# A hybrid encoder trunk on one core: the prologue in another order

## The reference

```python
c_act = jax.nn.silu(c)
for l in range(DEPTH):
    mod = c_act @ ada_w[l] + ada_b[l]
    sh1, sc1, gt1, sh2, sc2, gt2 = [m[:, None, :] for m in jnp.split(mod, 6, axis=-1)]
    h = rms_norm(x) * (1 + sc1) + sh1
    z = h @ w_in[l]
    ...  # z feeds latent attention with a rotary key, and a bidirectional RWKV-7 mixer
    x = x + gt1 * (jnp.concatenate([y_mla, y_rwkv], axis=-1) @ w_out[l])
    h = rms_norm(x) * (1 + sc2) + sh2
    x = x + gt2 * conv_ffn(h, ffn_w_up[l], ffn_conv_w[l], ffn_conv_b[l], ffn_w_down[l])
return rms_norm(x, final_norm)
```

## Time and profile before

| | us |
|---|---|
| median of 3 runs (lowest, highest) | 2013.53 (2013.17, 2016.87) |
| the profiled execution | 2015.64 |
| its span, first instruction to last | 2013.7 |
| TensorE's matmuls busy | 1702.9 (85%) |
| VectorE busy | 1066.8 (53%) |
| ScalarE busy | 726.9 (36%) |
| GpSimd busy | 293.2 (15%) |

### The profile page before, as it was taken

The page is one execution under the profiler, slowest core; times in us unless marked ns, Lnnn a source line. Parts: engine busy times, 40 slices in busy tenths (PEclk is TensorE's granted clock), DMA queues, the critical chain, the costliest instruction groups (busy, mean ns, idle before and its releaser), DMA issues.

```text
span 2013.7 us, 27787 instructions
## 1 busy us (share of the span) xinstructions
PE 1702.9 (85%) x11192; PEld 1259.4 (63%) x11192; DVE 1066.8 (53%) x1533; ACT 726.9 (36%) x1159; POOL 293.2 (15%) x124
## 2 busy tenths in 40 slices
PE   0897874888888899999989978568877989999997
PEld 0584432666655688887857834256655768888785
DVE  7254458777533776763333244677772254544333
ACT  1434233455442323232233343445545143232322
POOL 1242000000002122121223400000000222121120
PEclk9999895787788999999999989677788989999999
DMA  6254020000023345452213310000000312222222
GB/s 272 85 177 158 14 84 15 2 2 2 2 105 125 125 173 202 177 198 84 86 62 103 95 64 1 0 2 2 1 2 13 114 54 92 99 88 103 85 85 82
DMA packets 34651, 162.96 MB, mean 81 GB/s; under 512 B 3840, under 2 KB 4096, under 8 KB 25856
## 3 DMA queue, kind: packets, MB, share of 16 engines
q1 hardware_dynamic: 34560, 161.65, 22.7%
HBM read 159.54 MB, written 2.10 MB: 80 GB/s over the span
## 4 chain that ended last, share of the span: by engine, by line
PE 71%; DVE 14%; ACT 7%; issue 6%; DMA 1%; POOL 0%; DVEq 0%; SPq 0%; ACTq 0%; POOLq 0%
PE bank L483 12%; PE bank L485 12%; PE bank L484 12%; PE bank_pair L483 4%; PE bank_pair L485 4%; PE bank_pair L484 4%; DVE work L1316 2%; PE bank L769 2%; PE bank L770 1%; PE bank_pair L573 1%; PE bank L544 1%; PE bank L552 1%; PE bank L747 1%; PE bank L699 1%; PE bank L505 1%
## 5 line engine op out<-in xcount | busy, mean ns | idle before, releaser
L483 PE MATMUL bank<-work_parts,y_mix_parts 128*128 128x512 f32 x792 | 316.2, 399 | 24.1 <-DVE work_parts L1479 15.9
L485 PE MATMUL bank<-work_parts 128*128 128x512 f32 x792 | 314.9, 398 | 0.0
L1492 DVE TENSOR_TENSOR work_parts<-work,y_mix_parts 128x1024 fp32r<-128x1024 f32 x66 | 169.4, 2567 | 254.0 <-ACT y_mix_parts L869 253.9
L1695 POOL TENSOR_TENSOR proj_weights_parts<-proj_weights,proj_weights_hi 128x1024 fp32r<-128x1024 f32 x54 | 132.7, 2460 | 1072.0 <-ACT proj_weights_hi L863 996.2
L1700 POOL TENSOR_TENSOR work_parts<-work,y_mix_parts 128x1024 fp32r<-128x1024 f32 x66 | 160.3, 2429 | 616.1 <-ACT y_mix_parts L869 616.1
L869 ACT ACTIVATE y_mix_parts<-work 128x1024 fp32r<-128x1024 f32 x132 | 132.8, 1054 | 251.8 <-DMA work<-mlp_dram 251.8
L484 PE MATMUL bank<-work_parts,y_mix_parts 128*128 128x512 f32 x528 | 209.0, 396 | 0.0
L483 PEld LDWEIGHTS bank<-work_parts,y_mix_parts 128*128 128x128 f32 x792 | 150.2, 190 | 66.1 <-issue 24.7
L485 PEld LDWEIGHTS bank<-work_parts 128*128 128x128 f32 x792 | 150.3, 190 | 35.6
L483 PE MATMUL bank<-work_parts,proj_weights_hi 128*128 128x512 f32 x304 | 126.9, 417 | 27.0 <-DVE work_parts L1479 12.1
L485 PE MATMUL bank<-work_parts,proj_weights_parts 128*128 128x512 f32 x304 | 124.3, 409 | 0.0
(11 more groups left out here) (252 smaller groups left out, 3185.4 us busy)
## 6 DMA issues: line engine op xcount, KB each, us to landing
work<-mlp_dram SPq DMA_DIRECT2D x66, 1024.0 KB, 4.9
work<-ada_dram SPq DMA_DIRECT2D x64, 512.0 KB, 4.7
proj_weights<-tiles_dram SPq DMA_DIRECT2D x57, 512.0 KB, 3.6
x_res<-ada_dram SPq DMA_DIRECT2D x24, 512.0 KB, 4.9
mixer_inputs<-ada_dram SPq DMA_DIRECT2D x8, 512.0 KB, 15.2
x_res<-x_dram SPq DMA_DIRECT2D x2, 2048.0 KB, 13.7
work<-mlaw_dram SPq DMA_DIRECT2D x4, 640.0 KB, 4.4
out_dram<-x_res SPq DMA_DIRECT2D x8, 256.0 KB, 2.2
```

Source lines behind the costliest of these rows:

```text
L483: mm(out, w_hi, x_hi, start=start, stop=False)
L485: return mm(out, w_lo, x_hi, start=False, stop=stop)
L1492: TTT(MW_L[q][:, 1], MW_IN[q][:, 1], plain(MW_H[q][:, 1]), ALU.subtract).then_inc(msp_v.sem, msp_v.one("l1"))
L1695: pool.tensor_tensor(ring_l[s], ring[s], plain(ring_h[s]), ALU.subtract).then_inc(spl_q.sem, spl_q.one(f"t{s}"))
```

## The change

SyncE's queue starts with c and the first four blocks of the matrix; constants and x come next, then the other twelve blocks, the parameters, the three weight tiles, and the positions last. ScalarE makes the tanh first, then the whole norm of x, and splits the first two weight tiles only behind the norm's exponential. VectorE starts with the conditioning vector and the dots. The angles and the lane constants stand behind the rows of the first norm, ScalarE's sines behind the fourth result of the projection, and the sign of the sine behind the last operation on the mixer's gate. Nothing is left out or added but waits. The core of the diff:

```diff
@@ block.sync @@
+            sp.dma_start(CACT, c.partition_broadcast(P)).then_inc(c_in, 16)
+            for j in range(4):
+                sp.dma_start(ADA0[j], ada[0, j]).then_inc(ada0_in[0], 16)
             sp.dma_start(CST[:, :], cst).then_inc(const_in, 16)
-            sp.dma_start(POS_IN.bitcast(I32), pos.partition_broadcast(P)).then_inc(pos_in, 16)
-            sp.dma_start(CACT, c.partition_broadcast(P)).then_inc(c_in, 16)
-            for j in range(16):
+            sp.dma_start(X[:, :].rearrange("p (k t) -> p k t", k=KD), x).then_inc(x_in, 16)
+            for j in range(4, 16):
                 sp.dma_start(ADA0[j], ada[0, j]).then_inc(ada0_in[j // 4], 16)
-            sp.dma_start(X[:, :].rearrange("p (k t) -> p k t", k=KD), x).then_inc(x_in, 16)
+            sp.dma_start(PR[:, :], prm[0]).then_inc(prm_in, 16)
             for s in range(3):
                 sp.dma_start(ring[s], tiles[s]).then_inc(ring_in[s], 16)
+            sp.dma_start(POS_IN.bitcast(I32), pos.partition_broadcast(P)).then_inc(pos_in, 16)
@@ block.scalar @@
-            act.wait_ge(const_in, 16)
-            act.wait_ge(pro_v.sem, pro_v.at("s15", 0))
-            F(sin, sin, ACT.Sin).then_inc(pro_a.sem, pro_a.one("sin"))
-            F(cos, cos, ACT.Sin).then_inc(pro_a.sem, pro_a.one("cos"))
             act.wait_ge(c_in, 16)
             F(TANH_C, CACT, ACT.Tanh, scale=0.5).then_inc(pro_a.sem, pro_a.one("tanh"))
+            act.wait_ge(const_in, 16)
             act.wait_ge(x_in, 16)
+            def trig():
+                act.wait_ge(pro_v.sem, pro_v.at("s15", 0))
+                F(sin, sin, ACT.Sin).then_inc(pro_a.sem, pro_a.one("sin"))
+                F(cos, cos, ACT.Sin).then_inc(pro_a.sem, pro_a.one("cos"))
...
                 F(rs[1], rs[0], ACT.Exp, scale=-0.5).then_inc(nrm_a.sem, nrm_a.one("rstd"))
                 if h is False:
                     return
+                before_rows()
...
-                for t in range(2):
-                    split_tile(l, t)
-                act.wait_ge(lay_v.sem, lay_v.at("muc", l))
-                norm(2 * l, 0)
+                def first_two():
+                    for t in range(2):
+                        split_tile(l, t)
+                    act.wait_ge(lay_v.sem, lay_v.at("muc", l))
+                if l == 0:
+                    norm(0, 0, before_rows=first_two)
+                else:
+                    first_two()
+                    norm(2 * l, 0)
                 for j in range(4):
...
+                if l == 0:
+                    trig()
@@ block.vector @@
...
-            dve.wait_ge(pro_a.sem, pro_a.at("tanh", 0))
-            TSC(sin, sin, CST[:, K_SIGN:K_SIGN + 1], None, ALU.mult)
+            dve.sem_inc(x_ready.sem, KD)
+            x_ready.turn += KD
+            dve.wait_ge(c_in, 16)
+            dve.wait_ge(pro_a.sem, pro_a.at("tanh", 0))
             STT(CACT, TANH_C, 1.0, CACT, ALU.add, ALU.mult).then_inc(cact_done, 1)
...
+            dve.wait_ge(const_in, 16)
             dve.wait_ge(x_in, 16)
-            dve.sem_inc(x_ready.sem, KD)
-            x_ready.turn += KD
...
                 norm_rows(2 * l, 8, 0)
+                if l == 0:
+                    angles()
+                    lanes_ready()
...
                 TSC(mix(XG), mix(XG), 1.0, 0.5, ALU.add, ALU.mult).then_inc(in_v.sem, in_v.one("sxg"))
+                if l == 0:
+                    dve.wait_ge(pro_a.sem, pro_a.at("cos", 0))
+                    TSC(sin, sin, CST[:, K_SIGN:K_SIGN + 1], None, ALU.mult)
```

More of the change, by code:

```diff
@@ L263, in trunk @@
         pro_v = steps("pro_v", [f"s{i}" for i in range(16)])
-        pro_a = steps("pro_a", ["sin", "cos", "tanh"])
+        pro_a = steps("pro_a", ["tanh", "sin", "cos"])
         nrm_a = steps("nrm_a", [f"sq{k}" for k in range(KD)] + ["ln", "rstd"] + [f"h{k}" for k in range(KD)])
@@ L378, in _ @@
             for l in range(DEPTH):
-                sp.wait_ge(up_v.sem, up_v.before("a1", l * (NF // 2)))
-                sp.dma_start(PR[:, :], prm[l]).then_inc(prm_in, 16)
+                if l:
+                    sp.wait_ge(up_v.sem, up_v.before("a1", l * (NF // 2)))
+                    sp.dma_start(PR[:, :], prm[l]).then_inc(prm_in, 16)
                 if l == 0:
@@ L869, in split_mlp, with norm @@
                     F(MW_H[q][:, half], MW_IN[q][:, half], ACT.Identity).then_inc(msp_a.sem, msp_a.one(f"h{half}"))
-            def norm(n, h=True, between=lambda: None):
+            def norm(n, h=True, between=lambda: None, before_rows=lambda: None):
                 for k in range(KD):
@@ L1246, in _, with angles, pro @@
                 ada_cols(2 * j, j, ADA0[2 * j:2 * j + 2])
+            dve.wait_ge(const_in, 16)
             dve.wait_ge(x_in, 16)
-            dve.sem_inc(x_ready.sem, KD)
-            x_ready.turn += KD
[L1251 to L1254, removed]
-                dve.memset(VBR[p][:, 0:C], 0.0).then_inc(lane_v, 1)
+            def angles():
+                dve.wait_ge(const_in, 16)
+                dve.wait_ge(pos_in, 16)
+                two_pi = 2 * np.pi
+                p1 = 6.28125
+                p2 = float(np.round((two_pi - p1) * 2 ** 21) / 2 ** 21)
+                p3 = float(two_pi - p1 - p2)
+                turn, magic, limit = float(1 / two_pi), 1.5 * 2 ** 23, 3.1415925
+                n = [0]
+                def pro(ins):
+                    ins.then_inc(pro_v.sem, pro_v.one(f"s{n[0]}"))
+                    dve.wait_ge(pro_v.sem, pro_v.at(f"s{n[0]}", 0))
+                    n[0] += 1
+                ang, rnd = RS[:, 0:SEQ], RS[:, SEQ:2 * SEQ]
+                pro(dve.tensor_copy(ang, POS_IN.bitcast(I32)))
+                pro(TSC(ang, ang, CST[:, K_FREQ:K_FREQ + 1], None, ALU.mult))
+                for dst, quarter in ((sin, 0.0), (cos, 0.25)):
+                    pro(TSC(rnd, ang, turn, quarter, ALU.mult, ALU.add))
+                    pro(TSC(rnd, rnd, magic, None, ALU.add))
+                    pro(TSC(rnd, rnd, magic, None, ALU.subtract))
+                    pro(STT(dst, rnd, -p1, ang, ALU.mult, ALU.add))
+                    pro(STT(dst, rnd, -p2, dst, ALU.mult, ALU.add))
+                    pro(STT(dst, rnd, -p3, dst, ALU.mult, ALU.add))
+                    if quarter:
+                        TSC(dst, dst, float(np.pi / 2), limit, ALU.add, ALU.min).then_inc(pro_v.sem, pro_v.one("s14"))
+                        dve.wait_ge(pro_v.sem, pro_v.at("s14", 0))
+                        TSC(dst, dst, -limit, None, ALU.max).then_inc(pro_v.sem, pro_v.one("s15"))
+                    else:
+                        TSC(dst, dst, limit, -limit, ALU.min, ALU.max)
+                        n_ = n[0]
+                        assert n_ == 8
@@ L1257, in own, with lanes_ready @@
+            def lanes_ready():
+                dve.memset(XL[0:64, :], 0.0).then_inc(lane_v, 1)
+                dve.wait_ge(lane_v, 1)
+                dve.tensor_copy(XL[0:64, :].rearrange("p (a x) -> p a x", x=33)[:, :, 0], ones[0:64, 0:32]).then_inc(lane_v, 1)
+                for p in range(2):
+                    dve.memset(VBR[p][:, 0:C], 0.0).then_inc(lane_v, 1)
             def own(s, ins, name):
```

30 lines of the change are left out of this document (removed).

## The result

The changed kernel took 1997.26 us, the median of five runs (1990.97 to 2000.59), against 2016.44 for the kernel before in the same comparison (2013.17 to 2018.49): a ratio of 0.9904, 95% interval 0.9883 to 0.9926. That is 19.2 us less, between 14.9 and 23.6. The forecast was 1995, 18.45 less. The profiled execution took 1998.02 us against 2015.64, 17.62 less, with a span of 1996.1 us.

The account below looks back on a forecast made before the run. One chain up to TensorE's first projection at 66.73 us was taken as the bound: 4.4 (dots) + 1.4 (lane constants) + 13.0 (norm) = 18.8, less 0.35, is 18.45; 2013.53-18.45 = 1995.1, forecast 1995 us, range 1990 to 2001.

Parts of the forecast that it names:

- the lag: Prologue transfers: a landing comes about 1.9 us after the byte count says, bounds 0 and twice that.
- The norm: Ahead of the first projection: x's norm runs beside transfers and dots, ends at about 32, hiding 13.0 us.
- The rival in which it is not hidden: Prologue: x lands late or the squares still wait, the 13 us come back: 2008 us; chance 0.05.
- Transfers bind the dots: VectorE's dots: first group at 11.6, second waits for weights until 23.6; dots end 4.4 us earlier, collision included.
- The rival without this bound: Prologue: transfers don't bind, dots run without a pause from 11.6 to 33.0: 1986 us; chance 0.02.
- The collision: Last dots: GpSimd's two subtractions for the first weight tile still stretch a dot and a copy, 4.15 us, bounds 0 and 4.80.
- the rival's "met instead": Objection to the no-collision rival (1991 us, chance 0.09): subtractions would meet the two-input row operations behind the parameters instead.
- Lane constants: VectorE between dots and parameters: moving them behind the first norm's rows gains 1.40 us.
- The tight place: GpSimd's subtraction ahead of TensorE's fourth projection tile, delayed by angle operations: 0.35 us lost, bounds 0 and 0.7.
- Work laid into waits: First projections: sines, table loads and sign operation go into existing waits at no cost; uncovered 2.5, 1.28 and 0.5 us.
- The sign operation: Among the projections: about 0.5 us on VectorE, put into its wait of 1.23 at 116.79, costed at nothing.
- The two rivals with TensorE staying at 1.2 GHz: Projections: one tile at the lower clock, 2000.7 us, chance 0.12; clock down throughout, five tiles 2023 us, chance 0.04.

Follow-up runs that it names:

- finer waits: Changed kernel with one semaphore for each two weight blocks instead of each four, so a pair of dots waits for its own blocks; 1988.52 us in one run.
- both late edits together: Changed kernel with a semaphore per two weight blocks and the first two weight tiles loaded and split ahead of the norm; 1988.98 us, ratio 0.9877.

## Why the prediction was right

The mechanism held up to TensorE's start; the lag was mis-sized, and so was what the angles take among the projections, which had cover.

**The norm** was to be hidden whole, 13.0 us. It is: undone alone it costs 13.37, done alone it gives 12.99. The rival in which it is not hidden has fallen. The rest of the 20.25 is 1.27 from the lane constants and 6.0 from the dots' earlier end: 4.1 with ScalarE's sines and tanh out of their way, 1.85 with the angles.

**Transfers bind the dots.** Predicted: first group at 11.6, a wait of some 6 us, second group at 23.6. Measured: 10.45, 6.43 and 22.08. This is the term that was mis-sized ahead of TensorE's start. The lag of a landing behind the byte count had been taken as 1.9 from the first weight tile of before (its figures give 1.96), and the first 10 us at 269 GB/s. With the rates of after, 2.96 MB are in at 10 us and the 7.55 MB of the second group are due at 10+4.59/0.413 = 21.1: a lag of 1.0. x gives the same (5.45 MB due at 16.0, squares at 17.01), the first weight tile 1.2 (12.37 MB due at 32.8, split at 33.97; the positions no longer lie ahead of it, but the parameters now do). So 0.65 us of the miss is the first window's rate (0.27 MB more at 0.414 MB per us) and 0.9 the lag. Why the first window was faster and the lag shorter was not tried. The rival without this bound has fallen: the dots wait 6.43 us for a transfer, and with the angles in front a start 8.3 later cost 1.85.

**The collision** was taken at 4.15 and is (2.29-0.17)+(3.32-1.22) = 4.22; taken away, it gave 3.46, and 0.73 of the rest is the memset that took its place. The same kinds of operation were met, by luck of a few tenths of a us: finer waits moved it to others at nearly the same price, (2.19-0.17)+(2.17-0.18) = 4.0 (0.18 is that parameter operation in the trace after), much as the rival's "met instead" had it.

**Lane constants**: 1.4 taken, 1.27 measured. **Parameters** took 43.94-42.19 = 1.75, not 1.54.

Together: TensorE's start was put 18.8 earlier and came 20.25 earlier; the lag and the first rate are 1.5 of this, the parameters took 0.2 back.

**The tight place.** TensorE waits 0.51 for GpSimd ahead of the fourth tile where it waited 0.30, and the tile starts 67.85-46.48 = 21.37 behind the first, against 87.87-66.73 = 21.14: 0.23, with 0.35 taken. The question left open is answered: an angle operation, under 0.5 us by itself, takes 2.55 at 55.54, with a subtraction beside it, and two later ones 2.50 and 2.51. The rule of the Trainium skill quoted in the prediction (SBUF — State Buffer, section "Who interferes with whom"), that fast one-input operations hold the ports too, agrees with these rows. With the angles in front of the dots the wait was 0.18. Three operations were stretched where the prediction had allowed for one: the moved work ended at 72.09, which is 92.1 in the times of before, and not between 86.2 and 88.6. VectorE's idle stretch of 24.65 paid for all three.

**Work laid into waits.** Sines and table loads, of which there is one more than before (37 against 36), cost nothing (0.39 and 0.90 of their cover are left). The sign operation was priced at 0.5 against a cover of 1.23. It met a subtraction of GpSimd's, took 2.62, overran its cover and made the shift at 98.01 late: 18.8 us ahead of 116.79 and not 20. The step failed as written, and cost nothing, since the next shift, at 102.36, waits 2.82 and TensorE waits for neither.

**The clock.** The two rivals with TensorE staying at 1.2 GHz have fallen: after 19.46 us of idling the rise came some 5 us into the first tile (51.4 to 51.8), which VectorE paces anyway, and in the windows it is 1.00 from 55 on.

**From the start to the end.** 20.25 of an earlier start less 0.23 would be 20.0; the profiled pair shows 17.62. Up to the end of the projections, at 179, all of the 20.0 is there. No edit touches what follows, and there the lead drifts: with the traces matched matmul by matmul it is 22.2 at 305, 18.4 at 586, 20.3 at 1158 and 17.6 at the end (22.4, 18.8, 20.6 and 17.9 in the second trace of the changed kernel). The largest loss is in a stretch of many small matmuls, layer 0's attention and what follows, before and after:

```profile
304.00:585.00 281.00, 210.83 (x3088) 156.72 (x3088) 187.88 (x286) 132.62 (x266) 0.00 (x0) 0.75 0.01 2
```

```profile
282.00:566.60 284.60, 215.03 (x3088) 160.25 (x3088) 188.16 (x286) 133.10 (x266) 0.00 (x0) 0.73 0.01 2
```

The same 3088 matmuls took 281.0 us at a mean granted clock of 0.75 and 284.6 at 0.73. Elsewhere the lead grows again without an edit. From the first projection matmul to the last instruction the kernel before takes 2013.7-66.73 = 1947.0 us, the changed one 1949.6 and 1949.2, and the other versions between 1942.3 (both late edits together) and 1952.6 (x behind the sixteen blocks), so 2.4 us are within what this part varies by. Over the runs of the two comparisons with several runs each the means are 2014.8 for the kernel before (15 runs) and 1995.7 for the one after (11), 19.1 less, and the interval of the first comparison, 14.9 to 23.6, holds 20.0; so a small loss from the clock is neither shown nor excluded. That the profiled difference came so near to 18.45 is in part luck: the start came 1.45 earlier than forecast, and 2.4 were lost behind it. The forecast's 1995 against 1997.26 is mostly its base: 2013.53 was the median of three runs, 2016.44 that of five.

## What to carry to other kernels

Before a chain on one engine is shortened, count the bytes that its inputs need: here the dots began 12.35 us earlier and ended 6.0 earlier, and the last 8.3 us of the earlier start were worth 1.85, because the transfers stood right behind them, while the norm, a chain on other engines with all it needed landed early, gave 13. Work that moves into a wait must be priced with the collisions of its new place (2.6 us for an operation of 0.5), and what counts is then not its cover alone but whether the next instruction behind it had slack.

## What was not expected of the hardware

GpSimd's memset of 0.95 us held up a copy of two columns (0.90 for 0.17) but not a dot with two inputs (1.22). A parameter operation of 16 columns is held as long as a large one: 2.17 where the earlier trace rows have 0.10. And runs of one kernel on one chip differ by up to 11 us (1989.89 to 2001.24, at mean granted clocks of 0.902 and 0.894), over half of what this change is worth.
